# Moving data 32 bytes off the weights' grid in a float32r layer pair on one Trainium2 core

## Chip, core and metric

One core of one Trainium2 chip runs the whole program. The metric is the device time of one launch in microseconds; the kernel before takes 2131.46 us (median of 3 runs, 2130.79 to 2133.56).

## What is computed

256 tokens of width 1024 go through two blocks, everything in float32:

```
# block 1
n1 = rmsnorm(h);  proj = n1 @ w_in                 # q k v r, su sv, gates
h += (sig(ga)*(gla(...) @ w_a) + sig(gb)*(sgu(...) @ w_b)) @ w_out
n2 = rmsnorm(h);  q = n2 @ peer_wq                 # 8 heads, top 16 of 128x128 experts
a = gelu(n2 @ expert_u.T) * gates;  h += a @ expert_v   # 16384 experts
# block 2, for x = rmsnorm(h) and a context of 256 tokens
x += 0.5*g1*swiglu(mod(rmsnorm(x)))                # also for ctx
x += g2*merge(retention(x, ctx), fourier(x)) @ w_out
x += 0.5*g3*swiglu(mod(rmsnorm(x)))
return rmsnorm(x)
```

## The kernel before, in words

All weights come as one stream of chunks of 128 x 1024 float32 (512 KB). SyncE loads chunk c into slot c % 4 of `RAW` (L379). ScalarE rounds it to float32r in `WH` (`split_hi`, L510) and VectorE, or GpSimd in the stage of the query projection and in `pre` (L466), writes the rest to `WL` (L993). TensorE then makes three products for each float32 product: high by high, low by high, high by low. The activations are held as such pairs too.

Two forms of chunk matter.

- `feature_chunk` (L1660 on, through `product`, L1656 to L1658): the weights' 128 x 128 tile is stationary and the activations, 256 columns for 256 tokens or 512 where x and the context go together, are moving. One chunk is 8 tiles times 3 products, 24 matmuls.
- `token_chunk` and the expert `down` (L1689 to L1691, L1934 to L1936): the activation's 128 columns are stationary and 512 columns of the weights are moving.

The moving activations are `XHL` (halves `XH` and `XL`: the first projections, w_out, 32 rows of expert ups called `pre`, two more), `MH`/`ML` (branches), `XRP` (query projection), `XH2`/`XL2`, seen as `XH2_16` with 512 tokens or as `XH2_8` with 256 (second w_out and second FFN's up), `YRH`/`YRL` and `YFH`/`YFL` (output projections). The remaining 94 expert ups are `up_wide`: for each tile one matmul that moves `XHL[:, :, k, :]`, 2 x 256 columns with a step of 8192 bytes between the halves, against `WH` (L1920), and one that moves 256 columns of `XH` against `WL` (L1922). Each is followed by a `down` of 12 matmuls, whose stationary data are the gated rows `AH`/`AL`.

The order of the work is written out by hand for each engine, and semaphores order the engines; nothing is planned by a cost model. In the query projection and in `pre`, VectorE computes top-k. TensorE transposes its result (`SEL`, L1880) after 28 of the 32 `pre` chunks.

Places in SBUF are fixed by hand. `sb(name, shape, offset)` puts a tensor at `base + offset`, with `base` 16512, and without an offset behind the last one, rounded up to 32 bytes. `WH` and `WL` are at offsets 16384 and 32768, and every tile in them is a multiple of 512 bytes further. Modulo 128, with `base` a multiple of 128, the places in the kernel before are: `WH`, `WL`, `XHL`, `MH`, `ML`, `XH2`, `XL2`, `YRH`, `YRL`, `YFH`, `YFL`, `AH`, `AL`, `HIDH`, `HIDL` at 0, `XRP` at 64 (the tensors ahead of it have odd sizes), `ONES` at 64, `CS` at 32. "On the grid" below means equal to the weights modulo 128, "off the grid" another place.

Of the kernel before, what the change touches and what calls it, by code (L numbers as in the profile page):

```python
# [19 lines left out]
F32R = mybir.dt.float32r  # L20
# [5 lines left out]
P = 128  # L26
D = 1024
KB = D // P
T = 256
TT = T // P  # L30
# [127 lines left out]
def build(nc, a, out):  # L158

    ctx = ExitStack()  # L160
    with ctx:
        s = Sems(nc, ctx)
        base = 16512
        place = [0]

        def sb(name, shape, offset=None, dt=F32):
            size = 4
            for d in shape[1:]:
                size *= d
            if offset is None:  # L170
                offset = place[0]
            place[0] = offset + (size + 31) // 32 * 32
            return nc.alloc_sbuf_tensor_at(name, shape, dt, offset=base + offset)
# [3 lines left out]
        WH = sb("WH", [P, 4, 1024], dt=F32R)  # L177
        WL = sb("WL", [P, 4, 1024], dt=F32R)
        H = sb("H", [P, KB, T])
        XHL = sb("XHL", [P, 2, KB, T], dt=F32R)  # L180
        XH, XL = XHL[:, 0, :, :], XHL[:, 1, :, :]
        AHP = place[0]
        AH = sb("AH", [P, 2, T], dt=F32R)
        AL = sb("AL", [P, 2, T], dt=F32R)
        REG = place[0]
        G = sb("G", [P, NKEYS, T])
        CL = sb("CL", [P, NCOLS])
        MOD = sb("MOD", [P, MODB, 2])
        SCG = sb("SCG", [P, 3, KB, 2])
# [2 lines left out]
        IDP = sb("IDP", [P, P])  # L192
        EPSC = sb("EPSC", [P, 1])
        LGD = sb("LGD", [P, 4, 8])
        CS2 = sb("CS2", [P, KB, 2])
        CS = sb("CS", [P, KB, 32])
        RTOK = sb("RTOK", [P, 2, TT])
        assert base + place[0] <= nc.sbuf_usable_end
# [25 lines left out]
        MV = sb("MV", [P, TT, 2])  # L224
        TMPM = sb("TMPM", [P, 2, T])
        MG = sb("MG", [P, KB, T])
        XRP = sb("XRP", [P, 2, KB, T], dt=F32R)
        KEEP = REG + 131072 - 8192
        assert place[0] <= KEEP
        K12T = sb("K12T", [P, 2, P], KEEP)  # L230
        QT = sb("QT", [P, 4, T])
        assert place[0] <= REG + 131072
        MH = sb("MH", [P, KB, T], REG + 28672, dt=F32R)
        ML = sb("ML", [P, KB, T], dt=F32R)

        XRA = sb("XRA", [P, 2, KB, T], REG, dt=F32R)
# [28 lines left out]
        assert place[0] <= REG  # L265


        HX = sb("HX", [P, KB, 2 * T], 57344)
        XH2 = sb("XH2", [P, KB * 2 * T], REG, dt=F32R)
        XL2 = sb("XL2", [P, KB * 2 * T], dt=F32R)  # L270
        R2 = place[0]
# [42 lines left out]
        MG2 = sb("MG2", [P, KB, T], R3)  # L314
        TMP2 = sb("TMP2", [P, 2, T])
        DIST = sb("DIST", [P, 2, 4, T], 49152)
        IDENT2 = sb("IDENT2", [P, P], 73728)
        OST6 = sb("OST6", [P, TT, 6])
        OMV = sb("OMV", [P, TT, 2])
        SSUM = sb("SSUM", [P, TT, 2])  # L320
# [5 lines left out]
        DIAG = sb("DIAG", [P, KB, P], 49152)  # L326
        G3B = sb("G3B", [P, D])
        assert place[0] <= 57344
        Y1 = sb("Y1", [P, TT, D], 57344)
        SQT = sb("SQT", [P, TT, D])  # L330
        assert place[0] <= 73728
        HXT = sb("HXT", [P, TT, D], REG + 8192)
        LASTG = sb("LASTG", [P, D], REG + 24576)

        ps = ctx.enter_context(nc.psum_tensor("ps", [P, 8, 512], F32))

        def col(name, k):
            return CL[:, COLS[name] + k:COLS[name] + k + 1]


        X_, C_ = slice(0, T), slice(T, 2 * T)
        XH2_8 = XH2[:, 0:KB * T].rearrange("p (k t) -> p k t", k=KB)
        XL2_8 = XL2[:, 0:KB * T].rearrange("p (k t) -> p k t", k=KB)
        XH2_16 = XH2[:, :].rearrange("p (k t) -> p k t", k=KB)
        XL2_16 = XL2[:, :].rearrange("p (k t) -> p k t", k=KB)

# [11 lines left out]
        def early_row(g):  # L358

            return G[:, PRE_ROW - 16 + 2 * g:PRE_ROW - 14 + 2 * g, P:2 * P]  # L360

# [15 lines left out]
        def _(sp):  # L377
# [6 lines left out]
            load_x(0)  # L384
            sp.dma_start(CL[:, :], a["cols"]).then_inc(s["cols_landed"], 16)
            load(0, 0)
# [6 lines left out]
            for dst, name in ((WA2[:, :], "wa2b"), (UM[:, :], "umat"),  # L393
                              (BONES[:, :], "bones"), (WST[:, :, :], "wsT"), (BS[:, :], "bs"),
                              (LNG[:, :], "lng"), (LNB[:, :], "lnb"),
                              (K12T[:, :, :], "k12T"), (CS2[:, :, :], "cT"), (LGD[:, 0, :], "decays"),
                              (IDP[:, :], "ident")):
# [38 lines left out]
        def _(pool):  # L436
# [48 lines left out]
            pool.wait_ge(chunk_done, C0["up1"])  # L485
            pool.dma_start(HX[:, :, T:2 * T], a["ctxT"]).then_inc(s["ctx_landed"], 16)
            pool.dma_start(IDENT2[:, :], a["ident"]).then_inc(s["tables_landed"], 16)
            pool.wait_ge(s["norm_out"], (N_FINAL + 1) * KB)
# [12 lines left out]
        def _(act):  # L501
# [96 lines left out]
            for n, func in enumerate((ACT.Copy, ACT.Silu, ACT.Gelu_apprx_tanh) + 4 * (ACT.Sigmoid,)):  # L598
                for j in range(4):
# [4 lines left out]
                    if (n, j) == (1, 0):  # L604
                        act.wait_ge(s["cs_zeroed"], 1)
                        act.activation(CS[:, :, 0:2], CS2[:, :, :], ACT.Silu).then_inc(s["cs_ready"], 1)
                    if j == 0:
                        glu(n)
                    if n == 6 and j == 2:

                        act.wait_ge(s["ya_ready"], 1)
                        act.activation(MH[:, 0:4, :], OG[:, :, :], ACT.Copy).then_inc(s["y_hi"], 1)

            act.wait_ge(s["yb_ready"], 1)
            act.activation(MH[:, 4:8, :], PROJ[:, 8:12, :], ACT.Copy).then_inc(s["y_hi"], 1)

# [9 lines left out]
            def raw_hi(m):  # L626

                act.wait_ge(ring_evac, U_WOUT + m + 1)
                act.activation(XRP[:, 0, m, :], H[:, m, :], ACT.Copy, scale=col("norm2", m)).then_inc(s["xrp_hi"], 1)

# [33 lines left out]
            for i in range(PRE):  # L664
                c = C_PRE[i]
                if i and i + 2 < PRE:
                    split_hi(C_PRE[i + 2])
                act.wait_ge(chunk_done, c + 1)
                act.activation(G[:, PRE_ROW + i, :], ps[:, (U_PRE + i) % 4, 0:T],  # L669
                               ACT.Gelu_apprx_tanh).then_inc(ring_evac, 1)  # L670
# [36 lines left out]
            for n in range(UNITS):  # L707
                if n + 1 < UNITS:
                    hots(n + 1)
                act.wait_ge(s["onehot_used"], n + 3)  # L710
                act.activation(G[:, 0:PRE_ROW, 8 * n:8 * n + 8],
                               ps[:, 2 * (n % 2):2 * (n % 2) + 2, :].rearrange("p b (t i) -> p i (b t)", t=4)[:, 0:PRE_ROW, :],
# [12 lines left out]
            def pre_hi(i, it=None):  # L725
                if it is not None or i >= 2:

                    act.wait_ge(chunk_done, at(PC + 2 + i - 2 + 1, 4, it))
                src = G[:, PRE_ROW + i, :] if it is None else G[:, bass.ds(it * 4 + (PRE_ROW + i), 1), :]
                dst = AH[:, i % 2, :] if it is None else AH[:, i % 2, :].unsqueeze(1)  # L730
                act.activation(dst, src, ACT.Copy).then_inc(s["a_hi"], 1)

            def expert_hi(e, it=None):
                act.wait_ge(s["gated_ready"], at(e + 1, 4, it))

                act.wait_ge(chunk_done, at(PQ + 3 + 2 * (e - 2) + 1, 8, it) if e >= 2 else PQ + e + 1)
                src = G[:, e, :] if it is None else G[:, bass.ds(it * 4 + e, 1), :]
                dst = AH[:, e % 2, :] if it is None else AH[:, e % 2, :].unsqueeze(1)
# [78 lines left out]
            def ffn(n, up, down, width):  # L817
# [24 lines left out]
                for c in range(down + 22, min(down + 24, NCH)):  # L842
                    split_hi(c)

            norm(N_FFN1, HX[:, :, X_], TMP16[:, :, X_], RMS5[:, X_], XH2_16[:, :, X_],
                 (s["norm_out"], lambda k: N_FINAL * KB + k + 1), lambda k: MOD[:, k, 0:1])
# [3 lines left out]
            for k in range(KB):  # L850
                act.wait_ge(s["hx_ready"], k + 1)
                norm_square(N_MIX, k, HX[:, :, X_], TMP16[:, :, X_])
            norm_root(N_MIX, RMS5[:, X_])
            for k in range(KB):
                act.wait_ge(s["hx_ready"], KB + k if k else 1)
                norm_square(N_CTXMIX, k, HX[:, :, C_], TMP16[:, :, C_])
            for k in range(KB):
# [128 lines left out]
        def _(dve):  # L986
# [147 lines left out]
            for n in range(7):  # L1134
                for j in range(4):
# [3 lines left out]
            dve.wait_ge(s["y_hi"], 1)  # L1139
            dve.tensor_tensor(ML[:, 0:4, :], OG[:, :, :], MH[:, 0:4, :].bitcast(F32), ALU.subtract).then_inc(s["y_lo"], 1)  # L1140
            dve.wait_ge(s["yb_ready"], 1)
            dve.wait_ge(s["y_hi"], 2)
            dve.tensor_tensor(ML[:, 4:8, :], PROJ[:, 8:12, :], MH[:, 4:8, :].bitcast(F32),
                              ALU.subtract).then_inc(s["y_lo"], 1)
# [20 lines left out]
            def raw_lo(m):  # L1165

                dve.wait_ge(s["xrp_hi"], m + 1)
                dve.scalar_tensor_tensor(XRP[:, 1, m, :], H[:, m, :], col("norm2", m), XRP[:, 0, m, :].bitcast(F32),
                                         ALU.mult, ALU.subtract).then_inc(s["xrp_lo"], 1)
# [125 lines left out]
            def gated_rows(n):  # L1295

                dve.wait_ge(s["g_ready"], n + 3)
                g = G[:, PRE_ROW:NKEYS, 8 * n:8 * n + 8]
                rows = ps[:, 2 * (n % 2):2 * (n % 2) + 2, :].rearrange("p b (t i) -> p i (b t)", t=4)
# [23 lines left out]
            dve.wait_ge(s["row_summed"], GROUPS)  # L1323
            bada = CL[:, COLS["bada"]:COLS["bada"] + MODB].unsqueeze(2).to_broadcast([P, MODB, 2])
            step.link(dve.tensor_tensor(MOD[:, :, :], MOD[:, :, :], bada, ALU.add))
# [28 lines left out]
            for n, name in enumerate(("ffn1", "mix", "ffn2")):  # L1354
                sc = MOD[:, 24 * n + 8:24 * n + 16, :]
                dve.scalar_tensor_tensor(SCG[:, n, :, :], sc, 1.0,
                                         CL[:, COLS[name]:COLS[name] + KB].unsqueeze(2).to_broadcast([P, KB, 2]),
                                         ALU.add, ALU.mult)
# [120 lines left out]
            with dve.Fori(0, RH) as it:  # L1479
# [59 lines left out]
                for v in range(4):  # L1539
                    gain = CL[:, bass.ds(it * 4 + (COLS["gn"] + v), 1)]  # L1540
                    ins = dve.scalar_tensor_tensor(YT[:, v, :], ps[:, 6 + v // 2, (v % 2) * T:(v % 2) * T + T],
# [103 lines left out]
        def _(pe):  # L1645
# [152 lines left out]
            for j in range(KB):  # L1798
# [3 lines left out]
                for k in range(KB):  # L1802
                    if j == 0 and k % 4 == 0:
                        pe.wait_ge(s["y_lo"], k // 4 + 1)
                    w = slice(k * P, k * P + P)
                    dst = ps[:, (U_BRANCH + j) % 4, (k // 4) * T:(k // 4) * T + T]
                    ins = product(dst, WH[:, c % 4, w], WL[:, c % 4, w], MH[:, k, :], ML[:, k, :],
                                  k % 4 == 0, k % 4 == 3)
# [19 lines left out]
            for i in range(16):  # L1828
                bank_free(U_WQ + i)
                feature_chunk(C0["wq"] + i, ps[:, (U_WQ + i) % 4, 0:T], XRP[:, 0, :, :], XRP[:, 1, :, :],  # L1830
                              parts=None if i else s["xrp_lo"])
# [82 lines left out]
            def up_wide(e, c, it=None):  # L1914
# [3 lines left out]
                for k in range(KB):  # L1918
                    w = slice(k * P, k * P + P)
                    pe.matmul(both, WH[:, c % 4, w], XHL[:, :, k, :], start=(k == 0), stop=(k == KB - 1),  # L1920
                              skip_group_check=True)
# [374 lines left out]
```

## Time and profile before

| | before |
|---|---|
| median of 3 runs | 2131.46 us (2130.79 to 2133.56) |
| the profiled execution's own time | 2128.1 us |
| its span, first to last instruction | 2126.3 us |
| instructions | 35639 |
| TensorE busy (matmuls, weight loads) | 98%, 86% of the span |
| VectorE, ScalarE, GpSimd busy | 58%, 49%, 7% |
| HBM read | 341.76 MB, 161 GB/s over the span |

The profiled execution is 3.4 us under the median. Its span leaves out 1.8 us around the first and last instruction. A matmul's duration in the profile includes its way through the array, and the next one starts long before it ends. So what one matmul costs is the distance between starts: two rows of the timeline, divided by how many starts lie between them.

### The profile page before, as it was taken

The numbers are of one execution on the slowest core, as the hardware profiler recorded it, in microseconds if no ns is written. First come the engines' busy times: TensorE is split into PE (matmuls) and PEld (weight loads), VectorE is DVE, ScalarE is ACT, GpSimd is POOL, SyncE is SP. The second block draws the span as 40 slices with busy tenths as digits, with TensorE's granted clock in tenths as the row PEclk, the third lists the DMA queues.
The fourth block names the chain that finished last, engine by engine and source line by source line (L and its number), as shares of the span: only waits on it lengthen the run. The fifth ranks groups of instructions, "written<-read, shape, count | busy, mean of one in ns | idle before, by whom it ended". The sixth has DMA issues, their size and how long they took to land.

```text
span 2126.3 us, 35639 instructions
## 1 busy us (share of the span) xinstructions
PE 2081.3 (98%) x12718; PEld 1819.0 (86%) x12718; DVE 1232.0 (58%) x2082; ACT 1036.9 (49%) x1585; POOL 140.3 (7%) x82
## 2 busy tenths in 40 slices
PE   8999999999999999999999999999999999999998
PEld 6899999668888888888888888887888898899997
DVE  5457896986666666666665333323755554356554
ACT  6645644775555555555554222212543444336764
POOL 1001676000000000000000000000000000000000
PEclk9999999999999999999999999999999999999999
DMA  6435565886555555565543223322323345254564
GB/s 210 149 130 178 187 219 170 295 300 207 194 190 186 190 187 189 184 210 185 190 160 105 93 99 99 109 99 84 100 99 119 104 143 178 92 189 139 178 202 130
DMA packets 95669, 343.97 MB, mean 162 GB/s; under 512 B 11011, under 2 KB 11523, under 8 KB 95333
## 3 DMA queue, kind: packets, MB, share of 16 engines
q1 hardware_dynamic: 94196, 337.02, 47.2%
q0 software_dynamic: 1248, 5.57, 0.7%
q8 instruction: 56, 0.92, 0.2%
q10 hardware_dynamic: 144, 0.26, 0.0%
q14 instruction: 25, 0.20, 0.0%
HBM read 341.76 MB, written 1.05 MB: 161 GB/s over the span
## 4 chain that ended last, share of the span: by engine, by line
PE 90%; DVE 4%; ACT 2%; DMA 2%; POOL 1%; issue 1%; SPq 0%; ACTq 0%; DVEq 0%; POOLq 0%
PE ps L1656 16%; PE ps L1657 16%; PE ps L1658 16%; PE ps L1920 8%; PE ps L1934 6%; PE ps L1936 6%; PE ps L1935 6%; PE ps L1922 4%; DMA RAW<-in_wstream 2%; PE ps L1689 2%; PE ps L1690 2%; PE ps L1691 2%; PE ps L1898 2%; PE ps L1856 1%; PE ps L2165 1%; PE ps L2167 1%
## 5 line engine op out<-in xcount | busy, mean ns | idle before, releaser
L993 DVE TENSOR_TENSOR WL<-RAW,WH 128x1024 fp32r<-128x1024 f32 x517 | 625.2, 1223 | 414.9 <-ACT WH L510 409.4
L510 ACT ACTIVATE WH<-RAW 128x1024 fp32r<-128x1024 f32 x565 | 585.2, 1052 | 236.5 <-PE ps L1936 106.7
L1656 PE MATMUL ps<-XH,WH 128*128 128x256 f32 (+1 forms) x1200 | 382.6, 319 | 6.0 <-DVE XL L1022 3.6
L1658 PE MATMUL ps<-XH,WL 128*128 128x256 f32 (+1 forms) x1200 | 379.2, 316 | 0.0
L1657 PE MATMUL ps<-XL,WH 128*128 128x256 f32 (+1 forms) x1200 | 379.2, 316 | 0.0
L1920 PE MATMUL ps<-XHL,WH 128*128 128x512 f32 x752 | 268.6, 397 | 0.0
L1656 PEld LDWEIGHTS ps<-XH,WH 128*128 128x128 f32 x1200 | 229.2, 191 | 24.5 <-DVE XL L1022 4.3
L1657 PEld LDWEIGHTS ps<-XL,WH 128*128 128x128 f32 x1200 | 229.5, 191 | 14.5
L1658 PEld LDWEIGHTS ps<-XH,WL 128*128 128x128 f32 x1200 | 229.3, 191 | 14.2
L1922 PE MATMUL ps<-XHL,WL 128*128 128x256 f32 x752 | 210.9, 281 | 0.0
L1934 PE MATMUL ps<-WH,AH 128*128 128x512 f32 x512 | 202.5, 395 | 0.0
L1936 PE MATMUL ps<-WL,AH 128*128 128x512 f32 x512 | 200.9, 392 | 0.0
L1935 PE MATMUL ps<-WH,AL 128*128 128x512 f32 x512 | 199.9, 390 | 0.0
L1920 PEld LDWEIGHTS ps<-XHL,WH 128*128 128x128 f32 x752 | 141.3, 188 | 33.8
L1656 PE MATMUL ps<-XHL,WH 128*128 128x256 f32 x568 | 164.1, 289 | 4.2 <-DVE WL L993 2.8
L1657 PE MATMUL ps<-XHL,WH 128*128 128x256 f32 x568 | 161.5, 284 | 0.0
L1658 PE MATMUL ps<-XHL,WL 128*128 128x256 f32 x568 | 161.4, 284 | 0.0
L1922 PEld LDWEIGHTS ps<-XHL,WL 128*128 128x128 f32 x752 | 141.9, 189 | 3.6
L466 POOL TENSOR_TENSOR WL<-RAW,WH 128x1024 fp32r<-128x1024 f32 x48 | 118.9, 2485 | 150.4 <-ACT WH L510 150.3
L1656 PEld LDWEIGHTS ps<-XHL,WH 128*128 128x128 f32 x568 | 109.8, 193 | 11.1 <-ACT G L669 4.7
L1936 PEld LDWEIGHTS ps<-WL,AH 128*128 128x128 f32 x512 | 96.1, 188 | 23.1
L1934 PEld LDWEIGHTS ps<-WH,AH 128*128 128x128 f32 x512 | 96.1, 188 | 21.3
(340 smaller groups left out, 3348.6 us busy)
## 6 DMA issues: line engine op xcount, KB each, us to landing
RAW<-in_wstream SPq DMA_DIRECT2D x625, 512.0 KB, 3.4
ADB<-in_wstream SPq DMA_DIRECT2D x12, 512.0 KB, 4.8
H<-in_xT SPq DMA_DIRECT2D x4, 256.0 KB, 6.4
CTX<-in_ctxT POOLq DMA_DIRECT2D x1, 1024.0 KB, 5.9
HX<-in_ctxT POOLq DMA_DIRECT2D x1, 1024.0 KB, 6.0
DIST<-in_dist POOLq DMA_DIRECT2D x1, 1024.0 KB, 5.2
out<-Y SPq DMA_DIRECT2D x3, 256.0 KB, 2.6
MASK<-in_mask POOLq DMA_DIRECT2D x1, 512.0 KB, 3.9
```

The costliest lines, as they stand in the source:

```text
L466: pool.tensor_tensor(WL[:, c % 4, :], RAW[:, c % 4, :], WH[:, c % 4, :].bitcast(F32), ALU.subtract).then_inc(lo_ready, 1)
L510: act.activation(WH[:, slot, :], RAW[:, slot, :], ACT.Copy).then_inc(hi_ready, 1)
L993: dve.tensor_tensor(WL[:, slot, :], RAW[:, slot, :], WH[:, slot, :].bitcast(F32), ALU.subtract).then_inc(lo_ready, 1)
L1656: pe.matmul(dst, wh, xh, start=start, stop=False, skip_group_check=not check)
L1657: pe.matmul(dst, wh, xl, start=False, stop=False, skip_group_check=not check)
L1658: return pe.matmul(dst, wl, xh, start=False, stop=stop, skip_group_check=not check)
L1689: pe.matmul(dst, xh[:, k, t], WH[:, slot, w], start=(k == 0), stop=False)
L1920: pe.matmul(both, WH[:, c % 4, w], XHL[:, :, k, :], start=(k == 0), stop=(k == KB - 1), skip_group_check=True)
L1922: ins = pe.matmul(ps[:, e % 4, 0:T], WL[:, c % 4, w], XH[:, k, :], start=False, stop=(k == KB - 1), skip_group_check=True)
L1934: pe.matmul(dst, AH[:, e % 2, t], WH[:, c % 4, d], start=first, stop=False)
L1935: pe.matmul(dst, AL[:, e % 2, t], WH[:, c % 4, d], start=False, stop=False)
L1936: ins = pe.matmul(dst, AH[:, e % 2, t], WL[:, c % 4, d], start=False, stop=last)
```

## The change

It adds no instruction, takes none away, and changes no semaphore or order: only places in SBUF differ.

- `XHL` goes from between `H` and `AH` to behind `G`, at 32 bytes off the grid. Everything from `AH` on moves down by 16384 bytes, which keeps it where it was modulo 128. `HX`, `Y1` and `SQT`, which share `XHL`'s place later, go with it.
- `XRP` goes from 64 bytes off the grid to 32 off it, `MH` and `ML` from 0 to 32.
- `XH2_8` and `XL2_8` were the first halves of `XH2` and `XL2` and become tensors of their own at the same region, 32 bytes off. `XH2_16` stays on the grid, and so do `YRH`, `YFH`, `AH`, `AL`, `HIDH`.
- `HXT` and `LASTG` move by 256 and 512 bytes to make room. `CS2` moves. The constants behind `XHL` shift by 32 bytes: `ONES` and `IDP` from 64 to 96, `CS` from 32 to 0 modulo 128.

```diff
         H = sb("H", [P, KB, T])
-        XHL = sb("XHL", [P, 2, KB, T], dt=F32R)
-        XH, XL = XHL[:, 0, :, :], XHL[:, 1, :, :]
         AHP = place[0]
         AH = sb("AH", [P, 2, T], dt=F32R)
         AL = sb("AL", [P, 2, T], dt=F32R)
         REG = place[0]
         G = sb("G", [P, NKEYS, T])
+        OFF = 32
+        HOME = place[0] + OFF
+        XHL = sb("XHL", [P, 2, KB, T], HOME, dt=F32R)
+        XH, XL = XHL[:, 0, :, :], XHL[:, 1, :, :]
...
-        CS2 = sb("CS2", [P, KB, 2])
...
-        XRP = sb("XRP", [P, 2, KB, T], dt=F32R)
+        XRP = sb("XRP", [P, 2, KB, T], REG + 105472 + OFF, dt=F32R)
+        CS2 = sb("CS2", [P, KB, 2])
...
-        MH = sb("MH", [P, KB, T], REG + 28672, dt=F32R)
+        MH = sb("MH", [P, KB, T], REG + 28672 + OFF, dt=F32R)
...
-        HX = sb("HX", [P, KB, 2 * T], 57344)
+        HX = sb("HX", [P, KB, 2 * T], HOME)
...
-        IDENT2 = sb("IDENT2", [P, P], 73728)
+        IDENT2 = sb("IDENT2", [P, P], AHP)
...
-        Y1 = sb("Y1", [P, TT, D], 57344)
+        Y1 = sb("Y1", [P, TT, D], HOME)
...
-        HXT = sb("HXT", [P, TT, D], REG + 8192)
-        LASTG = sb("LASTG", [P, D], REG + 24576)
+        HXT = sb("HXT", [P, TT, D], REG + 8192 + 256)
+        LASTG = sb("LASTG", [P, D], REG + 24576 + 512)
...
-        XH2_8 = XH2[:, 0:KB * T].rearrange("p (k t) -> p k t", k=KB)
-        XL2_8 = XL2[:, 0:KB * T].rearrange("p (k t) -> p k t", k=KB)
+        XH2_8 = sb("XH2_8", [P, KB, T], REG + OFF, dt=F32R)
+        XL2_8 = sb("XL2_8", [P, KB, T], REG + 16384 + 256 + OFF, dt=F32R)
```

## Rows read from the trace of the kernel before

**Rows 1.** The page: busy time by engine, chain that ended last.

```profile
span 2126.3 us, 35639 instructions
...
PE 2081.3 (98%) x12718; PEld 1819.0 (86%) x12718; DVE 1232.0 (58%) x2082; ACT 1036.9 (49%) x1585; POOL 140.3 (7%) x82
...
PE 90%; DVE 4%; ACT 2%; DMA 2%; POOL 1%; issue 1%; SPq 0%; ACTq 0%; DVEq 0%; POOLq 0%
```

**Rows 2.** TensorE matmuls by line and form: busy, mean ns of one, idle before.

```profile
L1922 PE MATMUL ps<-XHL,WL 128*128 128x256 f32 x752 | 210.9, 281 | 0.0
...
L1657 PE MATMUL ps<-XHL,WH 128*128 128x256 f32 x568 | 161.5, 284 | 0.0
...
L1657 PE MATMUL ps<-XRP,WH 128*128 128x256 f32 x128 | 35.7, 279 | 0.0
...
L1657 PE MATMUL ps<-ML,WH 128*128 128x256 f32 x64 | 18.1, 283 | 0.0
```

**Rows 3.** Timeline, TensorE, 62 to 64 us: start, duration, XHL as moving data.

```profile
62.00 0.28 PE L1656 MATMUL ps<-XHL,WH 128*128 128x256 f32 x1
...
63.80 0.28 PE L1656 MATMUL ps<-XHL,WH 128*128 128x256 f32 x1
```

**Rows 4.** Timeline, TensorE, two chunks that read XRP, 20 and 18 starts apart.

```profile
212.94 0.28 PE L1656 MATMUL ps<-XRP,WH 128*128 128x256 f32 x1
...
215.21 0.28 PE L1658 MATMUL ps<-XRP,WL 128*128 128x256 f32 x1
...
249.81 0.28 PE L1656 MATMUL ps<-XRP,WH 128*128 128x256 f32 x1
...
251.93 0.28 PE L1656 MATMUL ps<-XRP,WH 128*128 128x256 f32 x1
```

**Rows 5.** Timeline, TensorE, one wide expert up, eight pairs of 512 and 256 columns.

```profile
576.82 0.39 PE L1920 MATMUL ps<-XHL,WH 128*128 128x512 f32 x1
...
577.16 0.40 PE L1920 MATMUL ps<-XHL,WH 128*128 128x512 f32 x1
...
579.28 0.40 PE L1920 MATMUL ps<-XHL,WH 128*128 128x512 f32 x1
```

**Rows 6.** Timeline, TensorE, an expert down behind a wide up, 12 matmuls.

```profile
579.63 0.40 PE L1934 MATMUL ps<-WH,AH 128*128 128x512 f32 x1
579.87 0.40 PE L1935 MATMUL ps<-WH,AL 128*128 128x512 f32 x1
...
582.41 0.39 PE L1920 MATMUL ps<-XHL,WH 128*128 128x512 f32 x1
```

**Rows 7.** Timeline, TensorE, expert downs with no wide up between, 5 starts apart.

```profile
567.83 0.39 PE L1934 MATMUL ps<-WH,AH 128*128 128x512 f32 x1
...
568.96 0.39 PE L1936 MATMUL ps<-WL,AH 128*128 128x512 f32 x1
```

**Rows 8.** Timeline, TensorE, plain float32: seven of 512 columns, eleven of 256.

```profile
1800.07 3.17 PE L2120 MATMUL ps<-DFTL,FT 128*128 128x512 f32 x7
...
1063.65 2.54 PE L1698 MATMUL ps<-TMP,ONES 128*128 128x256 f32 x11
```

**Rows 9.** By form, 1897.6 to 2059 us: the second w_out and second FFN up.

```profile
L1656 PE MATMUL ps<-XH,WH 128*128 128x256 f32 x416 | 119.6, 288 | 3.1 <-DVE XL L1022 2.4 <-DVE WL L993 0.5
```

**Rows 10.** Timeline around the slot transposes: VectorE's last top-k work, then TensorE.

```profile
344.63 4.08 DVE L1272 TENSOR_TENSOR SEL<-VAL,GSUM 128x128 f32<-128x128 f32 x2
...
356.27 0.82 PE L1880 MATMUL ps<-IDP,SEL 128*128 128x128 f32 x6
```

**Rows 11.** Stages (engine busy, then PEclk, DMA share, GB/s): pre, experts.

```profile
265.00:370.00 105.00, 103.40 (x882) 96.43 (x880) 83.73 (x281) 49.41 (x80) 77.56 (x32) 1.00 0.59 200
571.00:1106.00 535.00, 535.00 (x2675) 449.76 (x2674) 343.82 (x491) 289.81 (x491) 0.69 (x1) 1.00 0.56 188
```

**Rows 12.** The same view, the two later stretches at half clock.

```profile
145.00:151.80 6.80, 6.80 (x27) 5.90 (x28) 5.76 (x7) 0.00 (x0) 0.00 (x0) 0.50 0.45 154
1930.00:1933.50 3.50, 3.36 (x13) 3.05 (x14) 3.32 (x10) 2.37 (x6) 0.00 (x0) 0.52 0.00 0
```

More of the change, by code:

```diff
@@ L328, in build @@
         assert place[0] <= 57344
-        Y1 = sb("Y1", [P, TT, D], 57344)
+        Y1 = sb("Y1", [P, TT, D], HOME)
         SQT = sb("SQT", [P, TT, D])
-        assert place[0] <= 73728
-        HXT = sb("HXT", [P, TT, D], REG + 8192)
-        LASTG = sb("LASTG", [P, D], REG + 24576)
+        assert place[0] <= HOME + 16384
+        HXT = sb("HXT", [P, TT, D], REG + 8192 + 256)
+        LASTG = sb("LASTG", [P, D], REG + 24576 + 512)
         ps = ctx.enter_context(nc.psum_tensor("ps", [P, 8, 512], F32))
```

## Prediction

> **What bounds the kernel now.** I read the page first. TensorE's matmuls are busy for 98% of the span and hold 90% of the chain that ended last, with VectorE at 58% and ScalarE at 49% [rows 1]. So only what changes the distance between two matmul starts, or the few waits of TensorE, can move the time. The durations by form then show something odd: matmuls of one kind, 256 float32r columns against `WH`, take 284 ns from `XHL`, 283 from `ML`, and 279 from `XRP` [rows 2], and `XRP` is the one buffer off the grid (64 bytes). Durations overlap, so the timeline decides. From `XHL`, 15 starts take 1.80 us, 120.0 ns each [rows 3]. From `XRP`, one chunk has 20 starts in 2.27 us, 113.5 ns, and another 18 in 2.12 us, 117.8 ns [rows 4]; the chunks alternate between the two, which makes 115.6 on average. In the wide ups seven pairs take 2.46 us, 351.4 ns a pair, though the first took 340 (576.82 to 577.16) [rows 5]. The 12 matmuls of a down behind one take 2.78 us, 231.7 ns each, the first of them 240 [rows 6]. Where downs follow downs it is 1.13 us for 5, 226 ns [rows 7].
>
> What is the least? Plain float32 has six distances of 512 columns in 3.17 - 0.59 us (the last one's own 0.592 us lies in the 3.17), 430 ns, and ten of 256 in 2.54 - 0.38, 216 ns [rows 8]. That is 214 ns for 256 more columns, 0.836 ns per column and 2 ns once; float32r (226 against 120) takes 106 ns for 256 more, half. So plain float32 goes over the data twice, and one pass would cost 107 + 2 = 109 to 110 ns for 256 columns and 216 for 512. Against that, each float32r matmul with its weight load on the grid carries 10 to 11 ns more, whether it is 256 or 512 wide. An extra that doesn't grow with the columns belongs to the weight load beside it. I take it that the two reads get in each other's way, and that their places matter. That the place matters is a row (279 against 284); why is a guess.
>
> **What the change does to each form.** No instruction is added, removed or moved to another queue, and no wait is; the DMAs move the same bytes. All gain or loss is a distance between starts.
>
> (a) 256 columns that leave the grid: `XHL` 568 x 3, `MH` 64 x 3 [rows 2], `XH2_8` 416 x 3 [rows 9], together 3144 matmuls at 120.0. No row has a buffer 32 off. The ends are 109.5 below and, above, 133: the largest excess on any row is the 240 of a 512 matmul, 24 over its least of 216, and 109.5 + 24 is 133. I take 113.5, the faster of `XRP`'s two states, since `XRP` is the nearest row in kind (same line, same width, off the grid) and 32 lies no further from the grid than 64. Gain 3144 x 6.5 = 20.4 us; by the ends, 33.0 us gained or 41 lost.
>
> (b) `XRP` goes from 115.6 to the same 113.5: 384 x 2.1 = 0.8 us. Ends: 2.3 gained, 6.7 lost.
>
> (c) The wide ups, 752 pairs [rows 2], move from 351.4 to what `XHL` gives at 32. The ends are 109.5 + 216 = 325.5 and 240 + 120 = 360. I take 340, the best pair that a row shows: 752 x 11.4 = 8.6 us; ends 19.5 gained, 6.5 lost.
>
> (d) The 94 x 12 = 1128 matmuls of the downs behind them don't change places. Their excess over 226 is carried over from the up (the first is the slowest, and it fades), so with a calmer up I take half of it: 1128 x 2.9 = 3.2 us. Ends: 6.4 gained, and at 240 each 9.4 lost.
>
> (e) What could eat the gain. TensorE must not reach L1880 before VectorE has `SEL`. VectorE is done at 344.63 + 4.08 = 348.7, TensorE comes at 356.3 [rows 10], so 7.6 us of cover. Ahead of it since the top-k began lie (b) and 28 x 24 = 672 matmuls of (a): 0.8 + 4.4 = 5.2 us, inside the cover. At 109.5 it would be 2.3 + 7.1 = 9.4, and 1.8 would be lost as a wait. GpSimd's split takes 77.56 / 32 = 2.42 us a chunk [rows 11], under the 24 x 113.5 = 2.72 that a chunk would last, and under 2.63 at the least, so it still hides, with little left. In the experts VectorE and ScalarE are busy 343.8 and 289.8 of 535 us and the DMA share is 0.56 [rows 11]; a chunk some 4% shorter needs nothing there. For early chunks that wait for ScalarE or VectorE anyway I take off 1 us. The moved `HX`, `Y1`, `HXT`, `CS` and constants are read by VectorE, ScalarE or plain float32 matmuls, and `XRP`'s and `XH2`'s matmuls differ by place while TensorE was the limit; I set these at nothing, since TensorE's queue covers them except in the norms, where a few ns times some 60 instructions stay under 1 us either way.
>
> (f) The clock. From 145 to 151.8 and 1930 to 1933.5 us the granted clock was 0.5, the 1.2 GHz level, with matmuls of few columns or rows and a wait ahead [rows 12]. Times shift, so such a stretch may vanish or come up elsewhere: half of 6.8 + 3.5, up to 5 us either way, in the range and not in the sum.
>
> Sum: 20.4 + 0.8 + 8.6 + 3.2 - 1 = 32 us. The profiled execution took 2128.1 (span 2126.3 and 1.8 around it), so it would take 2096.1; it stood 3.4 under the median, hence **2099.5 us**.
>
> **Rivals.**
>
> Full relief (0.13). 32 bytes keep the two reads apart altogether. For it: the place matters, and there are 10.5 ns to be had. Against it: 64 bytes gave back at most 6.5. All lower ends together, 33.0 + 2.3 + 19.5 + 6.4 = 61.2, less 1 and the 1.8 at L1880: 58.4, so 2073. What decides is whether `XHL`'s distance is near 110. The Trainium skill, TensorE: Matmul & The Clock Gate, section Back-to-back issue gap, has columns / 2.4 + 2.5 ns at full clock for an isolated matmul, 109.2 at 256; the float32 rows agree with it per pass, the float32r rows on the grid don't.
>
> No effect (0.13). The place has no part in it: `XRP`'s chunks are also the ones with matmuls on `K12T` between them and with top-k on VectorE. Then (a) and (c) stay at 120 and 351.4, (b) too, and the time is 2131. Against it: `pre` chunks, too, run beside top-k with other matmuls between, and have the 284 of all `XHL` matmuls. The Trainium skill, SBUF — State Buffer, section SBUF: two separate sides, speaks against the whole change: only VectorE and GpSimd share a port, TensorE "never wait[s] on anyone", so by it an offset is worth nothing and the sum is 0; the 10.5 ns that a float32r matmul costs over a float32 pass, and `XRP`'s 279, are what it does not explain.
>
> Slower (0.12). The place is the wide ups: `XHL` is read there as 2 x 256 columns, and the rows already show that this pattern, on the grid, swings between 340 and more and spoils the down behind it. If 32 off makes every pair 360 and every down matmul 240, (c) and (d) lose 6.5 + 9.4 = 15.9. With 256 columns at `XRP`'s slow 117.8, (a) gives 6.9 and (b) loses 0.8: 9.8 us slower, 2141. It decides where (a) gives under 15.9, above 114.9 ns a matmul.
>
> **How the numbers follow.** The forecast has 0.62, with its own range from (a) at 117.8 and nothing in (c) and (d) (6.9 - 0.8 - 1 gained, 2126) to (a) at 111.5 with a pair at 333 (26.7 + 1.6 + 13.8 + 4.5 - 1 = 45.6, 2086). Full relief has 0.13, no effect 0.13, slower 0.12. The range takes in full relief and no effect and leaves out slower and what lies beyond: 2072 to 2134. A measurement of this kernel tells 0.2%, 4.3 us, from no change; faster by more than that are forecast and full relief, 0.75, the same 0.13, slower 0.12.
>
> **What would show it.** Right: `XHL`'s and `XH2_8`'s distances at one value near 113 to 114 or alternating with 118 from chunk to chunk, durations under 284, and the experts' stage (571 to 1106) shorter by some 12 us; `YRH`'s, the 512-column first FFN's and the heads' distances unchanged at 120 and 226. The wait at L1880 stays absent. Wrong: `XHL` at 120 (no effect), at 110 (full relief), or a wide pair over 351 or downs over 232 (slower). If the distances fall and the time does not, a wait of TensorE for `WL` or `SEL` has grown.

## The result, and the profile after

| | before | changed |
|---|---|---|
| median | 2131.68 us (4 runs, 2130.79 to 2133.56) | 2117.03 us (4 runs, 2116.32 to 2119.15) |
| profiled execution, its span | 2128.1, 2126.3 us | 2116.84, 2115.0 us |

The ratio is 0.9937 with a 95% interval from 0.9921 to 0.9953: 14.65 us faster, where 32 were forecast. The direction was right and the measured time lies inside the stated range of 2072 to 2134. The likeliest time, 2099.5, was not met: the gain is less than half of the forecast one.

The page of the changed kernel (lines are two further down than before) differs little from [rows 1]:

```profile
span 2115.0 us, 35639 instructions
...
PE 2071.4 (98%) x12718; PEld 1816.6 (86%) x12718; DVE 1233.0 (58%) x2082; ACT 1037.2 (49%) x1585; POOL 142.2 (7%) x82
...
PE 90%; DVE 5%; ACT 2%; DMA 2%; POOL 1%; issue 1%; SPq 0%; ACTq 0%; DVEq 0%; POOLq 0%
```

TensorE is 98% busy before and after, and the same chain ends last. The forms, answering to [rows 2], hardly moved: `XHL` with 256 columns fell from 284 to 283 ns and `XRP` stayed at 279.

```profile
L1924 PE MATMUL ps<-XHL,WL 128*128 128x256 f32 x752 | 211.9, 282 | 0.0
...
L1659 PE MATMUL ps<-XHL,WH 128*128 128x256 f32 x568 | 161.0, 283 | 0.0
...
L1659 PE MATMUL ps<-XRP,WH 128*128 128x256 f32 x128 | 35.8, 279 | 0.0
```

These means take in stretches at half clock, more of them after (below). In `pre` alone (265 to 370 us before, 268 to 372 after), at full clock throughout, the durations did fall, by about as much as the distances. Before, then changed:

```profile
L1657 PE MATMUL ps<-XHL,WH 128*128 128x256 f32 x256 | 72.4, 283 | 0.0
```

```profile
L1659 PE MATMUL ps<-XHL,WH 128*128 128x256 f32 x256 | 71.4, 279 | 0.0
```

The timeline of the changed kernel's TensorE (start, duration) has the forms of [rows 3], of [rows 5, 6] and of the second FFN's up:

```profile
93.20 0.28 PE L1658 MATMUL ps<-XHL,WH 128*128 128x256 f32 x1
...
96.00 0.28 PE L1658 MATMUL ps<-XHL,WH 128*128 128x256 f32 x1
...
578.46 0.39 PE L1936 MATMUL ps<-WH,AH 128*128 128x512 f32 x1
...
581.19 0.40 PE L1922 MATMUL ps<-XHL,WH 128*128 128x512 f32 x1
...
583.98 0.39 PE L1936 MATMUL ps<-WH,AH 128*128 128x512 f32 x1
...
2014.20 0.28 PE L1658 MATMUL ps<-XH,WH 128*128 128x256 f32 x1
...
2015.95 0.28 PE L1658 MATMUL ps<-XH,WH 128*128 128x256 f32 x1
```

From `XHL`, 24 starts take 2.80 us, 116.7 ns each, where they took 120.0. Behind an earlier wide up, the down's 12 matmuls take 2.73 us, 227.5 each, where they took 231.7. In the next wide up (581.19 to 583.98) eight pairs take 2.79 us, 349 a pair. From `XH2_8` 15 starts take 1.75 us, 116.7 each. So the distances fall in each of these forms, by some 3 to 4 ns a matmul. They don't in `XRP`, as the table shows.

For the whole program I use one figure per form, in this section and the next: the mean of all distances from a matmul of that form to the next start, at full clock, without those over 1.25 times the form's median (pauses between chunks).

| form, count | before | changed | gain |
|---|---|---|---|
| `XHL`, 256 columns, 1704 | 119.9 ns | 116.9 | 5.1 us |
| `MH`/`ML`, 192 | 120.0 | 117.8 | 0.4 |
| `XH2_8`, 1248 | 120.0 | 116.7 | 4.1 |
| `XRP`, 384 | 115.6 | 117.0 | -0.5 |
| wide pair, 752 | 234.8 + 116.5 | 230.7 + 118.3 | 1.7 |
| downs behind it, 1128 | 231.8 | 227.8 | 4.5 |
| `XH2_16` with 256, `YRH`, `YFH` | 119.9 to 120.0 | 119.9 to 120.0 | 0 |
| 512 columns on the grid | 226.7 | 226.8 | 0 |

They add up to 15.3 us, and the medians differ by 14.65. The two profiled executions differ by 11.3 only. The stages view at half clock shows a part of the reason:

```profile
66.30:73.10 6.80, 5.87 (x27) 5.90 (x28) 5.68 (x9) 2.33 (x5) 0.00 (x0) 0.50 0.56 168
144.80:155.00 10.20, 10.20 (x40) 8.85 (x41) 6.82 (x8) 0.52 (x2) 0.00 (x0) 0.50 0.31 103
165.30:168.70 3.40, 3.40 (x16) 3.40 (x17) 2.06 (x2) 1.14 (x2) 0.00 (x0) 0.50 0.42 149
1923.20:1926.60 3.40, 3.40 (x14) 3.06 (x15) 3.22 (x8) 2.62 (x5) 0.00 (x0) 0.50 0.00 0
```

These are 6.8 + 10.2 + 3.4 + 3.4 = 23.8 us at 0.50, the 1.2 GHz level, in the changed kernel's execution, against 10.3 in that of before [rows 12]. 13.5 us more at half clock, with columns going at half their rate, can cost up to 6.8 us of the gain in this one execution. Whether that belongs to the change is asked below.

### The profile page after: what moved, and what is told of

It reads as the page before. It is cut to its first block, busy times and chain, and to the rows that moved or that the text cites. A ratio compares the mean times of both kernels' runs of the same rounds, so it can differ in the third digit from the quotient of the medians.

```text
span 2115.0 us, 35639 instructions
## 1 busy us (share of the span) xinstructions
PE 2071.4 (98%) x12718; PEld 1816.6 (86%) x12718; DVE 1233.0 (58%) x2082; ACT 1037.2 (49%) x1585; POOL 142.2 (7%) x82
## 3 DMA queue, kind: packets, MB, share of 16 engines
q0 software_dynamic: 1248, 5.57, 0.8%
## 4 chain that ended last, share of the span: by engine, by line
PE 90%; DVE 5%; ACT 2%; DMA 2%; POOL 1%; issue 1%; SPq 0%; ACTq 0%; DVEq 0%; POOLq 0%
PE ps L1658 16%; PE ps L1660 16%; PE ps L1659 16%; PE ps L1922 8%; PE ps L1937 6%; PE ps L1938 6%; PE ps L1936 5%; PE ps L1924 4%; PE ps L1691 2%; PE ps L1692 2%; PE ps L1693 2%; DMA RAW<-in_wstream 2%; PE ps L1900 1%; PE ps L2169 1%; PE ps L2167 1%; PE ps L2168 1%
## 5 line engine op out<-in xcount | busy, mean ns | idle before, releaser
L1936 PEld LDWEIGHTS ps<-WH,AH 128*128 128x128 f32 x512 | 96.1, 188 | 20.5
```

Of the source, the lines that this page charges most:

```text
L1936: pe.matmul(dst, AH[:, e % 2, t], WH[:, c % 4, d], start=first, stop=False)
```

## The experiments

All edits are in the places alone, except where said. "OFF" is the constant of the change.

**Only the layout, without the offset.**

```diff
-        OFF = 32
+        OFF = 0
```

> The changed kernel with OFF = 0: its layout, but every moved buffer back on the grid. Theory A (the offset against the weights sets the distance between matmul starts): XHL, MH, XRP and XH2_8 at 120.0 ns, the wide pair near 351, the downs behind near 231.8, so 2131 to 2134 us. Rival B (the new places as such matter, not the 32 bytes): distances stay at 117, pair 349, 2117. Rival C (the extra half-clock stretches of the changed kernel come with its early layout, not with the faster matmuls): half clock at 66 and 165 us here too; by theory A they come with the shifted times and need not show.

Measured: 2132.87 us (11 runs), ratio to before 1.0006 (0.9998 to 1.0015). `XHL` 119.9, `MH` 119.9, `XRP` 119.7, `XH2_8` 120.0, wide pair 351.3, downs 231.7. TensorE's timeline has 15 starts in 1.80 us:

```profile
92.07 0.28 PE L1660 MATMUL ps<-XHL,WL 128*128 128x256 f32 x1
...
93.87 0.28 PE L1660 MATMUL ps<-XHL,WL 128*128 128x256 f32 x1
```

Rival B falls: the move as such is worth nothing, and the 32 bytes are all of it. On C: this execution was at half clock for 6.8 us from 68.6, and for 3.4 from 150.5, 167.6 and 375.8 each, so the stretch near 66 us came without faster matmuls too.

**Other offsets for all moved buffers.** The same edit with OFF = 64, 96, 128.

> OFF = 64 for all moved buffers. Theory A1 (a distance is a property of the offset; the old XRP's 115.6 ns is what 64 bytes give): 256-column matmuls at 113.5 and 117.8, mean 115.6, 4.6 us less than at 32 over 3144 matmuls, and XRP back at 115.6; 2112 to 2114 us if the wide ups stay at a pair of 349. Rival A2 (what old XRP showed belonged to its stage): XHL and XH2_8 near 117 or 120.

> OFF = 96. Theory A with a pattern that repeats after 128 bytes and is even about 0: the same as 32 bytes, 117 ns for 256 columns. If the gain grows with distance in one direction only, near 113.

> OFF = 128. If the pattern repeats after 128 bytes: as with OFF = 0, 120.0 ns and a pair of 351. If it repeats only after 256 or more, another value between 109.5 and 120.

At 64, 2124.22 us (7 runs, ratio 0.9966, 0.9953 to 0.9979), and `XHL` took 117.5 ns, not 115.6; `XRP` 117.2. A1 falls in its mean. Both of the old `XRP`'s values do occur at 64, though: outside the half clock, 6 of 141 chunks of the four moved forms run at 113.3 ns, and most others at 117.8. One of the six, `XHL` with 15 starts in 1.70 us:

```profile
132.68 0.28 PE L1658 MATMUL ps<-XHL,WH 128*128 128x256 f32 x1
...
134.38 0.28 PE L1658 MATMUL ps<-XHL,WH 128*128 128x256 f32 x1
```

At 96 (one run, 2133.48 us) `XHL` is back at 119.9, in the trace 15 starts in 1.80 us:

```profile
92.00 0.28 PE L1659 MATMUL ps<-XHL,WH 128*128 128x256 f32 x1
...
93.80 0.28 PE L1659 MATMUL ps<-XHL,WH 128*128 128x256 f32 x1
```

At 128 (one run, 2122.37 us) it is 118.8 and not the 119.9 of 0, so two places 128 bytes apart aren't alike. "Modulo 128", by which the places of the buffers were described and the prediction argued, isn't the pattern. The old `XRP` lay at offset 182976 with the weights at 16384: 166592 bytes apart, which is 64 modulo 128 but 192 modulo 256.

**Is it the offset against the weights?**

```diff
-        base = 16512
+        base = 16512 + 32
```

> The kernel before with base 16512 + 32: every tensor moves by 32 bytes, the weights too, so nothing moves against anything else. Theory A (the offset of the moving data against the weights counts): all as before, XHL 120.0, XRP 115.6, wide pair 351, near 2131 us. Rival D (the place of the moving data as such counts, its position on a fixed grid of SBUF): XHL, MH and XH2_8 near 117 as in the changed kernel, and with the others near 2110.

Nothing changed: `XHL` 119.9, `XRP` 115.6, pair 351.3, downs 231.7, one run at 2132.99 us, and the kernel before beside it at 2132.72. In the trace 15 starts take 1.80 us:

```profile
92.02 0.28 PE L1657 MATMUL ps<-XHL,WH 128*128 128x256 f32 x1
...
93.82 0.28 PE L1657 MATMUL ps<-XHL,WH 128*128 128x256 f32 x1
```

Rival D falls: a buffer's own address doesn't count, only its distance from other tensors. Which tensor that is, this run doesn't show, since all of them moved. I take it to be the weights, the other data that these matmuls read. That other engines' accesses set the distance is less likely. In the kernel before, `XHL` has 119.9 ns in `pre`, where VectorE is busy for 83.7 and GpSimd for 77.6 of 105 us [rows 11], and `XH2_8` has 120.0 with GpSimd idle and VectorE at 34.3 of 60 us:

```profile
1940.00:2000.00 60.00, 60.00 (x502) 60.00 (x501) 34.29 (x43) 42.30 (x54) 0.00 (x0) 1.00 0.57 188
```

**The rest of 256 bytes.** OFF = 192, 160, 224.

> OFF = 192. The old XRP stood 192 from the weights modulo 256 (64 only modulo 128). If the pattern repeats after 256 bytes (OFF = 128 gave 118.8, not 120, so not after 128), the old 113.5 and 117.8, mean 115.6, belong to 192: XHL, MH, XRP, XH2_8 at 115.6. If XRP's 115.6 was its stage's, XHL and XH2_8 elsewhere.

> OFF = 160, for the scan. Measured so far, XHL's distance: 120 at 0, 117 at 32, 117.5 at 64, 120 at 96, 118.8 at 128. Smooth between 128 and 192: 117 to 118. A value of 120 would say that each 96 bytes or so the two reads meet again.

> OFF = 224, which is 32 below the grid modulo 256. If the pattern is even about 0: 117 as at 32. If not: between 115.6 and 120.

All offsets together (ns; the pair is its two distances; the last column is eight pairs and twelve downs, one expert):

| OFF | `XHL` | `MH` | `XRP` | `XH2_8` | wide pair | down | one expert |
|---|---|---|---|---|---|---|---|
| 0 | 119.9 | 119.9 | 119.7 | 120.0 | 351.3 | 231.7 | 5.59 us |
| 32 | 116.9 | 117.8 | 117.0 | 116.7 | 349.1 | 227.8 | 5.53 |
| 64 | 117.5 | 117.8 | 117.2 | 117.8 | 349.6 | 229.1 | 5.55 |
| 96 | 119.9 | 120.0 | 119.8 | 120.0 | 351.0 | 229.7 | 5.56 |
| 128 | 118.8 | 118.7 | 119.3 | 118.7 | 349.3 | 226.6 | 5.51 |
| 160 | 118.3 | 117.3 | 118.6 | 117.3 | 348.0 | 226.9 | 5.51 |
| 192 | 114.2 | 113.3 | 115.4 | 117.7 | 352.8 | 229.2 | 5.57 |
| 224 | 118.4 | 118.4 | 118.5 | 118.3 | 347.3 | 229.4 | 5.53 |

192 gives what the old `XRP` had, now in `XHL` and `MH`. For 256 columns the grid and 96 are the slowest places, and 192 is the fastest, but for `XH2_8` in this execution. The gain is not the same on both sides of 0 (32 against 224) and doesn't grow with distance. The wide ups prefer other places than the 256-column matmuls: 192 is the worst but the grid for an expert. Each row is from one execution. Offsets from 256 on weren't tried. Nor are 64 and 192 as far apart as their means: both have chunks at 113.3 and at 117.8, 6 of 141 at 64 and about half at 192. `XL2_8` lies 16384 + 256 bytes behind `XH2_8` in all these kernels, and at OFF = 0 the matmuls on both are at 120.0, so there 256 is like 0.

At 192 there are two distances again, now in two buffers. TensorE's timeline, first `XHL`, then `XH2_8`:

```profile
92.00 0.28 PE L1658 MATMUL ps<-XHL,WH 128*128 128x256 f32 x1
...
93.70 0.28 PE L1658 MATMUL ps<-XHL,WH 128*128 128x256 f32 x1
...
1964.35 0.28 PE L1658 MATMUL ps<-XH,WH 128*128 128x256 f32 x1
...
1966.12 0.28 PE L1658 MATMUL ps<-XH,WH 128*128 128x256 f32 x1
```

15 starts take 1.70 us (113.3 ns) in the first and 1.77 us (118.0) in the second. Single times: 2123.87 us at 192, 2117.61 at 160 (level with 32), 2128.06 at 224.

A sum of distances gives the time only within several us. Worked out as for 32, it is some 11 us gained at 64, where the medians show 6.9 (before beside it 2131.08). There the mean granted clock was 0.992 over the 7 runs and 0.994 over those of before, some 9 us more at half clock, which can cost half of that.

**What picks one of the two distances.** In the kernel before, one more score matmul between the chunks that read `XRP`:

```diff
-                for tt in range(TT):
+                for tt in (0, 0, 1):
```

> The kernel before with three score matmuls of 128 columns (the first one twice, into the same place) instead of two behind each query chunk; nothing moves. The chunks of old XRP alternate between 113.5 and 117.8 ns. State theory (a matmul's distance depends on a phase that the matmuls ahead leave behind, and what stands between two chunks sets it): the alternation changes, all chunks alike or in another order. Rival (it alternates with the weights' slot, or with what GpSimd and VectorE do in every other chunk): the same alternation, every second chunk at 117.8. 16 more matmuls of about 110 ns cost 1.8 us.

The alternation is gone: but for two chunks at and behind a stretch of half clock (232.6 us), every chunk of `XRP` runs at 113.3 to 113.5 ns, and the form's mean fell from 115.6 to 114.0. The one run took 2132.57 us (before beside it 2130.78). The third chunk and the fourth, 15 starts in 1.70 us each:

```profile
216.67 0.28 PE L1656 MATMUL ps<-XRP,WH 128*128 128x256 f32 x1
...
218.37 0.28 PE L1656 MATMUL ps<-XRP,WH 128*128 128x256 f32 x1
...
220.46 0.28 PE L1656 MATMUL ps<-XRP,WH 128*128 128x256 f32 x1
...
222.16 0.28 PE L1656 MATMUL ps<-XRP,WH 128*128 128x256 f32 x1
```

In the kernel before, the third chunk has 15 starts in 1.77 us:

```profile
216.12 0.28 PE L1656 MATMUL ps<-XRP,WH 128*128 128x256 f32 x1
...
217.89 0.28 PE L1656 MATMUL ps<-XRP,WH 128*128 128x256 f32 x1
```

Slot, VectorE and GpSimd do the same work in both kernels, so the rival falls. A chunk's distance depends on the offset and on a state that what went before leaves behind. What this state is inside the engine, no run shows. The program alone doesn't fix it: in two executions of one kernel with `MH` at 192 (the mixed one below), `MH` has 21 starts in 2.47 us (117.6 ns) in the first and in 2.38 us (113.3) in the second:

```profile
166.00 0.28 PE L1658 MATMUL ps<-MH,WH 128*128 128x256 f32 x1
...
168.47 0.28 PE L1658 MATMUL ps<-MH,WH 128*128 128x256 f32 x1
```

```profile
166.04 0.28 PE L1658 MATMUL ps<-MH,WH 128*128 128x256 f32 x1
...
168.42 0.28 PE L1658 MATMUL ps<-MH,WH 128*128 128x256 f32 x1
```

**Part of the change alone.** `XHL` at 32, the rest at 0:

```diff
-        XRP = sb("XRP", [P, 2, KB, T], REG + 105472 + OFF, dt=F32R)
+        XRP = sb("XRP", [P, 2, KB, T], REG + 105472, dt=F32R)
...
-        MH = sb("MH", [P, KB, T], REG + 28672 + OFF, dt=F32R)
+        MH = sb("MH", [P, KB, T], REG + 28672, dt=F32R)
...
-        XH2_8 = sb("XH2_8", [P, KB, T], REG + OFF, dt=F32R)
-        XL2_8 = sb("XL2_8", [P, KB, T], REG + 16384 + 256 + OFF, dt=F32R)
+        XH2_8 = sb("XH2_8", [P, KB, T], REG, dt=F32R)
+        XL2_8 = sb("XL2_8", [P, KB, T], REG + 16384 + 256, dt=F32R)
```

> The changed kernel with only XHL at 32 and MH, XRP, XH2_8 at 0. Theory A: XHL 117, the wide pair 349, the downs 227.8 as with all moved; MH and XH2_8 back at 120.0, XRP 119.7. XHL's part is then 1704 x 3.0 + 752 x 2.2 + 1128 x 4.0 = 11.3 us, of the 15.5 that all distances of the change add up to. If buffers act on one another beyond the next few matmuls, other values.

Each form came as expected: `XHL` 116.9, pair 349.1, downs 227.8; `MH` 120.0, `XH2_8` 120.0, `XRP` 119.8. The one time, 2126.61 us, is 5.2 under the median of the kernel before beside it (2131.8), where the distances say 11.3 less 1.6 for `XRP`, 9.7; its own execution was at half clock for 20.5 us between 51 and 2100 us, against 10.3 before. One run can't settle 5 us here (the spread is below).

**All 256-column data at 192.** This also moves `XH2_16`, `YRH`, `YFH` and `HIDH`.

```diff
-        REG = place[0]
-        G = sb("G", [P, NKEYS, T])
-        OFF = 32
+        REG = place[0] + 192
+        G = sb("G", [P, NKEYS, T], REG)
+        OFF = 0
```

> Everything from REG on, and XHL behind it, lies 192 bytes off the weights, so also XH2_16, YRH and YFH, which the change left on the grid. Theory A (offset modulo 256, with a state that is carried from matmul to matmul): every 256-column form at 113.4 or at 117.7, YRH, YFH and XH2_16 with 256 columns too (they were 120.0), the wide pair 352.8 and the downs 229.2 as at OFF = 192. 1824 matmuls that were at 120 gain 2.3 to 6.6 ns: 4 to 12 us against OFF = 192, so 2112 to 2120. Rival: 512 columns moving off the grid lose as the wide ups do (they would leave 226.7), 2.6 us per ns.

2124.71 us (12 runs), ratio to before 0.9969 (0.9957 to 0.9981), slower than the change. Both sides of the expectation came true at once. `YRH` and `YFH` fell to 113.4, `XH2_8` to 114.1, `XH2_16` with 256 columns to 116.4, and `XHL`, at the same offset as with OFF = 192, had 116.4 in place of 114.2: it ran more chunks in the slower of the two states, 117.8. But 512 columns read off the grid rose from 226.7 to 233.3 (`XH2_16`) and 231.9 (`HIDH` and the last down together). TensorE's timeline, six starts of 512 columns in 1.40 us, then 15 of 256 in 1.69:

```profile
1150.20 0.40 PE L1658 MATMUL ps<-XH,WH 128*128 128x512 f32 x1
...
1151.60 0.40 PE L1658 MATMUL ps<-XH,WH 128*128 128x512 f32 x1
...
1850.02 0.28 PE L1658 MATMUL ps<-YFH,WH 128*128 128x256 f32 x1
...
1851.71 0.28 PE L1658 MATMUL ps<-YRH,WH 128*128 128x256 f32 x1
```

1104 x 6.6 and 791 x 5.2 ns are 11.4 us lost, 7.3 of them in `XH2_16`. Against these 7.3, its 256-column matmuls gained 1248 x 3.5 ns = 4.4 us, so that keeping `XH2_16` on the grid is worth some 3 us to the change. All distances of this kernel together say 13.8 us under the kernel before, and the medians show 7.1; where the rest went isn't settled.

**Each buffer at the offset that suits it.** `XHL` at 32, the others at 192:

```diff
-        XRP = sb("XRP", [P, 2, KB, T], REG + 105472 + OFF, dt=F32R)
+        XRP = sb("XRP", [P, 2, KB, T], REG + 105472 + 192, dt=F32R)
...
-        MH = sb("MH", [P, KB, T], REG + 28672 + OFF, dt=F32R)
+        MH = sb("MH", [P, KB, T], REG + 28672 + 192, dt=F32R)
...
-        HXT = sb("HXT", [P, TT, D], REG + 8192 + 256)
+        HXT = sb("HXT", [P, TT, D], REG + 8192 + 192)
...
-        XH2_8 = sb("XH2_8", [P, KB, T], REG + OFF, dt=F32R)
-        XL2_8 = sb("XL2_8", [P, KB, T], REG + 16384 + 256 + OFF, dt=F32R)
+        XH2_8 = sb("XH2_8", [P, KB, T], REG + 192, dt=F32R)
+        XL2_8 = sb("XL2_8", [P, KB, T], REG + 16384 + 192, dt=F32R)
```

> The changed kernel with XHL left at 32 and MH, XRP, XH2_8 and XL2_8 at 192. Theory A: XHL 117, pair 349, downs 227.8 as in the changed kernel; MH 113.3, XRP 115.5, XH2_8 113.4 or 117.7 by the state that it falls into: between 1 and 5 us under the changed kernel's 2117. If the values at 192 came from XHL's being there too, MH and XH2_8 at 117.

> XHL at 32, MH, XRP, XH2_8 and XL2_8 at 192, once more. By the distances (XH2_8 3.3 ns under the changed kernel over 1248 matmuls, XRP 1.1 over 384) 4.5 us under the changed kernel in the same rounds, 2111 to 2115; if the distances do not carry to the end, no difference.

> The changed kernel once more, for its spread beside the kernel before and the mixed one on one chip. Distances as in its first profile (XHL 116.9, pair 349.0, downs 227.8, XH2_8 116.7). If the 13.7 us more of half clock in its first profile belong to the change, again some 24 us at half clock between 51 and 2100 us; if they are chance, another figure between 10 and 27. Median 2115 to 2119.

The mixed kernel took 2114.49 us (6 runs, ratio 0.9933, 0.9914 to 0.9952) and again 2115.42 (6 runs, 0.9923, 0.9896 to 0.995). The changed one beside it took 2117.58 (6 runs, 0.9944, 0.9928 to 0.996). In both mixed profiles `XH2_8` fell to 113.4, where OFF = 192 had given 117.7 (`XL2_8` and what ran ahead differ too), and `XRP` to 115.9 and 115.6; `MH` took 117.8 in one and 113.4 in the other. `XH2_8` of the first, 15 starts in 1.70 us:

```profile
2000.17 0.28 PE L1658 MATMUL ps<-XH,WH 128*128 128x256 f32 x1
...
2001.87 0.28 PE L1658 MATMUL ps<-XH,WH 128*128 128x256 f32 x1
```

By distances that is 1248 x 3.3 + 384 x 1.2 = 4.6 us under the changed kernel. The median of all 12 mixed runs is 2114.8 and that of the 10 changed ones 2117.2, but the mixed runs spread from 2105.9 to 2121.5, and the intervals overlap. The distances are shown to be better, the time is not shown to be.

The second profile of the changed kernel has the same distances (`XHL` 116.8, pair 349.1, downs 227.8, `XH2_8` 116.7), but for `MH` (116.7 after 117.8). The half clock is another:

```profile
66.30:73.10 6.80, 4.12 (x35) 4.15 (x36) 5.45 (x8) 4.74 (x9) 0.00 (x0) 1.00 0.32 90
146.00:149.40 3.40, 3.40 (x15) 3.17 (x16) 3.30 (x4) 0.00 (x0) 0.00 (x0) 0.50 0.40 122
1919.00:1930.00 11.00, 9.51 (x66) 8.09 (x66) 8.15 (x16) 9.05 (x13) 0.00 (x0) 1.00 0.12 39
```

Between 51 and 2100 us it had one stretch, 3.4 us at 0.50. So the 23.8 us of the first profile don't come with the change each time, and over its ten runs the mean granted clock was 0.994, as over those of before. This execution took 2114.19 us, 2.65 less than the first, though 20.4 us less at half clock could be worth 10.2. A second source works against it here: the stage between the first one-hot matmul (370.6 us before) and the first down (484.2), in which TensorE waits for the weights' DMA among others. It took 113.6 us before, 111.7 in the changed kernel and 114.9 in its second profile. At OFF = 96 it took 120.3, with 3.4 us at half clock in it and 8.1 us of waiting for `RAW`'s DMA, against 3.4 before. So the same kernel on nearly the same distances differs by some microseconds from one execution to the next.

## Why the prediction was right or wrong

*What bounds the kernel* held: the distances between starts moved the time, and their sum, 15.3 us, is near what the medians show, 14.65. That they agree so well is in part luck, since at 64 and with all data at 192 the sum is 4 and 7 us above the medians' difference. *That place matters* held: OFF = 0 and OFF = 32 differ only in the offset and lie 16 us apart.

Of the 16.7 us between the forecast 32 and the 15.3 that the distances give, 10.8 are step (a), 6.9 step (c) and 1.3 step (b); step (d) and the 1 us taken off in (e) go the other way, by 1.3 and 1. The experts' stage became 6.3 us shorter, not 12.

*Step (a) failed, in its size.* It took 113.5 ns for 32 bytes from the faster state of `XRP`, as "the nearest row in kind". The measured figure is 116.9 for `XHL` and 116.7 for `XH2_8`: 9.6 us instead of 20.4. `XRP` was near in kind but not in place. I had reduced all places modulo 128 and so read 64 where it was 192 modulo 256, I took 64 to bound 32, and I took the faster of two states as if it would last. At 64 the runs show 117.5 on average and at 96 nothing is left. Whole chunks at 113.3 were seen at 192 (about half of them) and 64 (few), and at none of the other six offsets, 32 among them. How much of the difference between 64 and 192 is the place and how much the state, these runs don't separate. The trace of before held two places only, and two points carry no curve: the middle of 109.5 and 120 was all that could be taken from it without a scan.

*Step (b) had the wrong sign*: `XRP` was the one buffer at the best place, and the change took it away, 0.5 us lost for 0.8 gained in the forecast.

*Step (c)* took the best pair on a row, 340, for all pairs. In the kernel before, 340 was no value for all eight pairs of a wide up: the first pair took 341.9 ns on average over the 94 ups, and the other seven places 349 to 361. In the changed kernel the first is the slowest, 356.1, and the last five take 346.7. The mean became 349.0, 1.7 us instead of 8.6. *Step (d)* was right in kind: the downs didn't move, and their excess over 226.7 fell from 5.1 to 1.1 ns, 4.5 us for 3.2.

*Step (e)* held as far as it was tried: no wait appeared at the slot transposes (L1880, now L1882), where VectorE is done at 352.9 us and TensorE comes at 357.4, so that 4.5 of the 7.6 us of cover are left, and GpSimd still hid. *Step (f)* was right in kind and kept out of the sum rightly, but its 5 us were too few: the first profile had 13.5 us more at half clock, worth up to 6.8, the second 6.9 less than that of before.

*Rivals.* Full relief came at no offset: the best settled distance, 113.3 ns, is still 4 over the 109.5 of one float32 pass. The formula of the Trainium skill, TensorE: Matmul & The Clock Gate, section Back-to-back issue gap, gives 109.2 at 256 columns, which no float32r matmul of any run here reached. No effect fell with 0.9937, and with the runs at OFF = 0 and 32, which differ in nothing but an offset: the distance goes from 119.9 to 116.9 ns. The Trainium skill, SBUF — State Buffer, section SBUF: two separate sides, says that TensorE never waits on anyone. That sentence is about engines contending at SBUF's ports. The prediction read from it that an offset is worth nothing, and this reading is what the runs refute; whether TensorE waits for another engine here, or its own two reads hinder each other, no run shows. Slower had the right place and the wrong sign, the wide ups and their downs got better at 32; yet its mechanism is real elsewhere, since 512 columns at 192 cost 6.6 ns each.

My cause, a weight load and a moving read that hinder each other by their places, fits the base + 32 run (only relative places count), but no run took the weight load away, and none moved the weight buffer alone against everything else. It stays argued.

## What to carry to other kernels

Measure distances between matmul starts at full clock, not mean durations of the whole program, for each buffer that feeds TensorE. With float32r, where they differ at the same width, scan the buffer's offset against the weights over 256 bytes in steps of 32, for each width apart, before forecasting from one neighbour. In this kernel 256 columns are mostly best at 192 and worst on the grid and at 96; 512 are better on the grid than at 192, the only other place tried for them (the wide ups apart); and a gain of 3 to 6% per 256-column matmul (116.9 and 113.3 ns against 120) is at stake. And since the value also depends on what ran before, take the mean over a whole stage, not the best row, and a second execution.

## What the runs showed that was not expected

- A float32r matmul of 256 columns has no single price at one offset: 113.3 or 117.8 ns at 192 and at 64, held over whole chunks. One more matmul of 128 columns between chunks ended their alternation in `XRP`, and two executions of one kernel can differ in it (`MH`, 117.6 and 113.3).
- `XHL`'s distance over the offset has two dips (at 32 and 64, and at 192, with 0, 96 and 128 above them) and is not symmetric.
- At half clock the excess is gone: chunks of `XHL`, `MH` and `XH2_8` run at 213 to 214 ns at every offset, 256 columns at 1.2 GHz being 213.3.
- The granted clock's half stretches between 51 and 2100 us came to 3.4 us in one execution and 23.8 in another of the same kernel on the same work.
